# GpSimd announces the end of the projection stage ahead of its rope gathers, and the logits are cleared behind the meeting

## What is computed

```python
z = rmsnorm(x, norm1_g) @ w_in                       # the projection, IN_WIDTH columns
z_q, z_kv, z_kr, z_u, z_v, z_ga, z_gb = jnp.split(z, IN_SPLITS, axis=-1)
q_lat, q_rope, c_kv, k_rope = mla_project(z_q, z_kv, z_kr, pos, ...)
o_lat = attend(q_lat, q_rope, c_kv, k_rope)          # prompt rows: causal; sample rows: over the cache too
...
def step(carry, pages):                              # sample attention, over the pages of the cache
    ck = cache_ckv[pages]
    kr = cache_krope[pages]                          # the rows that the "rope gathers" fetch
    s = mla_scores(q_lat, q_rope, ck, kr)
...
g_logit = (xt @ w_rg) + b_rg                         # router logits: the tile `logits` holds these and e_logit
```

## Time and profile before

| | |
|---|---|
| time, median of 3 runs | 1983.03 us (1980.97 to 1990.81) |
| the profiled execution | 1982.07 us, of which the span is 1980.3 us |
| PE busy | 1816.0 us (92% of the span) |
| DVE, ACT, POOL busy | 750.4, 456.2, 311.3 us |
| PE idle ahead of its first matmul behind the first meeting | 9.10 us |
| POOL's four drains at the meetings | 2.692 to 13.335 us |

### The profile page before, as it was taken

The page is one execution under the profiler, slowest core; times in us unless marked ns, Lnnn a source line. Parts: engine busy times, 40 slices in busy tenths (PEclk is TensorE's granted clock), DMA queues, the critical chain, the costliest instruction groups (busy, mean ns, idle before and its releaser), DMA issues.

```text
span 1980.3 us, 28999 instructions
## 1 busy us (share of the span) xinstructions
PE 1816.0 (92%) x11436; PEld 1238.7 (63%) x11436; DVE 750.4 (38%) x1687; ACT 456.2 (23%) x1002; POOL 311.3 (16%) x430
## 2 busy tenths in 40 slices
PE   7989999999979999999999997999898888898884
PEld 5678888888845656756666664565565555565551
DVE  3343334444423334334555555675322311111116
ACT  3122211111113233223344343212210111111013
POOL 1034311111110000000111103333321211111100
PEclk9999999999989999999999998999798999998997
DMA  7112215565620000026999995544899999999976
GB/s 221 45 66 76 76 60 210 212 214 214 225 87 1 1 1 1 1 65 196 289 304 299 300 303 192 203 143 156 304 408 417 418 415 411 416 405 402 400 326 264
DMA packets 107022, 432.90 MB, mean 219 GB/s; under 512 B 25216, under 2 KB 30752, under 8 KB 77184
## 3 DMA queue, kind: packets, MB, share of 16 engines
q1 hardware_dynamic: 86704, 330.02, 44.6%
q0 software_dynamic: 20160, 101.24, 15.4%
q10 hardware_dynamic: 48, 0.13, 0.0%
HBM read 388.12 MB, written 63.66 MB: 228 GB/s over the span
## 4 chain that ended last, share of the span: by engine, by line
PE 34%; DMA 17%; DVE 2%; ACT 1%; issue 0%; SPq 0%; POOLq 0%; DVEq 0%; ACTq 0%; PEldq 0%
DMA arena<-in_w_up_dram 16%; PE psum L1424 8%; PE psum L1162 6%; PE psum L1292 6%; PE psum L1173 5%; PE psum L1189 3%; PE psum L1443 1%; PE psum L1275 1%; PE psum L1180 1%; PE psum L1317 1%; DMA arena<-in_w_down_dram 1%; DMA arena<-y_rows 0%; DVE arena L2567 0%; PE psum L1282 0%; PE psum L1397 0%
## 5 line engine op out<-in xcount | busy, mean ns | idle before, releaser
L935 PE MATMUL psum<-arena 128*128 128x256 f32 x1792 | 392.6, 379 | 2.5 <-DVE arena L2126 2.1
L935 PEld LDWEIGHTS psum<-arena 128*128 128x128 f32 x1792 | 337.7, 189 | 55.7 <-issue 5.4
L1424 PE MATMUL psum<-arena 128*64 128x256 f32 (+1 forms) x2048 | 280.1, 407 | 65.8 <-DMA arena<-in_w_up_dram 64.0
L1424 PEld LDWEIGHTS psum<-arena 128*64 128x64 f32 (+1 forms) x2048 | 200.3, 153 | 135.5 <-issue 79.5
L1443 PE MATMUL psum<-arena 128*64 128x512 f32 (+1 forms) x512 | 131.3, 595 | 2.5 <-DMA arena<-in_w_down_dram 2.5
L2514 DVE TENSOR_TENSOR arena<-arena,psum 128x256 f32<-128x256 f32 x36 | 15.2, 423 | 310.6 <-ACT arena L1726 310.6
L1162 PEld LDWEIGHTS psum<-arena 128*128 128x128 f32 x1024 | 113.7, 142 | 29.8 <-issue 27.9
L1162 PE MATMUL psum<-arena 128*128 128x128 f32 x1024 | 127.5, 277 | 0.2 <-DVE arena L2204 0.2
L1292 PE MATMUL psum<-arena 128*128 128x512 f32 x256 | 114.3, 599 | 1.3 <-ACT arena L1659 1.3
L1624 ACT COPY arena<-psum 128x512 f32<-128x512 f32 x128 | 72.1, 589 | 171.6 <-PE psum L1162 171.6
L1936 POOL DMA_INDIRECT y_rows<-arena x36 | 40.7, 1131 | 403.5 <-DVE arena L2523 399.7
(11 more groups left out here) (341 smaller groups left out, 2277.0 us busy)
## 6 DMA issues: line engine op xcount, KB each, us to landing
arena<-in_w_gate_dram SPq DMA_DIRECT2D x64, 1024.0 KB, 13.6
arena<-in_w_up_dram SPq DMA_DIRECT2D x64, 1024.0 KB, 20.3
arena<-in_w_down_dram SPq DMA_DIRECT2D x64, 1024.0 KB, 22.3
arena<-in_w_in_dram SPq DMA_DIRECT2D x8, 2048.0 KB, 11.7
z_act<-arena SPq DMA_DIRECT2D x64, 256.0 KB, 2.1
rope_turned<-arena SPq DMA_DIRECT2D x32, 512.0 KB, 4.8
arena<-rope_turned SPq DMA_DIRECT2D x64, 256.0 KB, 11.2
arena<-z_act SPq DMA_DIRECT2D x8, 2048.0 KB, 7.7
```

Source lines behind the costliest of these rows:

```text
L935: last = mm(out[:, 0:256], x[:, k, :], w[:, k, :], start=(k == 0), stop=(k == 3))
L1424: last = mm(bank(2 + u)[rows, DE * x:DE * x + DE], xg_t[u][:, k, rows], w_e[slot][x][:, k, :], start=(k == 0), stop=(k == KD - 1))
```

## The change

POOL's stream: the drain and its increment of `ends` are moved from behind the 32 gathers and the wait for all stores to ahead of the first gather; only the wait `ends >= 4` stays behind. DVE's stream: the clearing of `logits` is moved from ahead of DVE's `stage_end` to behind it.

```diff
             pool.wait_ge(b_mm[0], groups_done(sched, ("G1", NTP))[0])
             pool.wait_ge(b_mm[1], groups_done(sched, ("sR", 0))[1])
+            pool.drain().then_inc(ends, 1)
             for n in range(NCH):
                 if n >= 2:
                     pool.wait_ge(rk_t, n - 1)
                 off = bass.IndirectOffsetOnAxis(ap=page_int[:, n:n + 1].bitcast(U32), axis=0)
                 pool.indirect_dma_start(kr_raw[n % 2].rearrange("p r c -> p (r c)"), None, kr_g, off).then_inc(c_in[n % 2], 16)
             for u in range(2):
                 pool.wait_ge(rk_mv[u], 16 * PRE)
-            stage_end(pool, 1)
+            pool.wait_ge(ends, 4)
```

```diff
                 for p in range(NTP // 2):
                     z_pair(b, p)
+            stage_end(dve, 1)
             step(V.memset(logits, 0.0))
-            stage_end(dve, 1)
```

## The result

The changed kernel takes 1972.12 us (median of 8 runs, 1968.89 to 1978.67) against 1986.85 us (median of 8 runs, 1980.97 to 1991.09) for the kernel before, on the same chips: a ratio of 0.9939, 95% interval 0.9925 to 0.9954. That is 12.1 us faster, between 9.1 and 14.9 us. The ratio is not the quotient of the two medians, which differ by 14.7 us. The forecast was 1973.0 us and 9.8 us.

A forecast was written before the change was run, and what follows sets the result against it. PE's 9.10 us idle at the projection's end, held by POOL alone, was taken as on the path; 7.3 us (meeting) + 2.5 us (clock) = 9.8 us off gave 1973.0 us, range 1968.5 to 1981 us.

The forecast's parts named there:

- Who holds the meeting, and what is late next: End of projection: POOL alone holds PE, DVE is next; PE starts 7.3 us earlier and idles 1.8 us.
- The clock: First K group behind the meeting: clock stays at full, group takes 3.60 instead of 6.11 us, another 2.5 us.
- The rival that it falls anyway: Behind the meeting: the clock still drops, only 7.3 us gained, 1975.7 us or something between; chance 0.16.
- The clearing of the logits: DVE, behind the meeting: its 0.60 us run while PE makes the first two K units, so are covered.
- w_uv: Start of V at 557.0 us: weights land at 555.9 us, margin 1.1 us, costed at nothing.
- The drain ahead of the gathers: POOL, before the first gather: drain of 2.692 to 13.335 us delays it; 22.7 us of cover, costs nothing.
- The gain reaches the end: Everything behind the meeting hangs on counts of engines' work and moves along; second meeting some 9.8 us earlier.
- rival 3: Experts: the 9.8 us are given back at a wait for weights, time 1983.0 us as before; chance 0.07.
- The sum against the median: Whole kernel: 9.8 us off the median of three runs, 1983.03 us, gives 1973.2 us; 1973.0 us predicted.

The follow-up runs named there:

- the early drain: Kernel before, with POOL's drain put between the last gather and the wait for the stores; 0.9979, 4.2 us faster.
- POOL's half: Kernel before, with only POOL's drain and announcement moved ahead of the gathers, logits still cleared ahead of DVE's drain; 0.9969, then 0.9952.
- the kernel that used it up: Changed kernel, with DVE announcing ahead of its last turn and PE waiting at the meeting neither for the others nor for `z_ev`; 0.9940.
- PE kept busy: Kernel before, with 9 idle matmuls on PE between its last product and the meeting, results unused; 0.9999, both times.
- DVE's half: Kernel before, with only the clearing of the logits moved behind the meeting, POOL announcing behind the stores as before; 1.0009.
- DVE late: Changed kernel, with five clearings of the logits ahead of DVE's drain; 0.9978, 4.4 us faster than before.

## Why the prediction was right, and where not

- **Who holds the meeting, and what is late next.** Right: POOL alone before; DVE with the change; the stall 1.78 us (1.8 foreseen), the meeting 7.32 us nearer (7.3). The split of POOL's lateness into stores and drain is shown by the early drain: 2.8 us for the drain. DVE's drain lasted 1.551 us where the prediction took 0.017 to 0.322 us, at no cost, since it ran beside the transposes and ended 0.06 us behind them.
- **The clock.** Right in the stage for this stall: 2.40 us (2.5 foreseen), in all three traces. The rival that it falls anyway did not happen at 1.78 us, but did once of two at 2.47 us, so its chance was not misplaced. The prediction rested on one row, the stall of 2.12 us at 585.44 us in which the clock stayed at full. At or behind that same stall it fell in four of the 14 traces, so the row was one outcome of two, and proved less than I took from it. The Trainium skill, "TensorE: Matmul & The Clock Gate", section "What's actually happening", says that the window runs free of the kernel; the two executions of POOL's half, equal in the stall and different in the clock, agree with this. What I drew from it, that even a stall of 1.8 us can be followed by a group at half rate, no trace shows: it did not happen in three executions with 1.78 us. That the 2.4 us reach the end isn't shown: the kernel with the clock alone kept measured 0.2 us, twice, and lost 1.7 us of the 2.4 again some 28 us later in both traces.
- **The clearing of the logits.** Right: hidden behind the meeting, 0.69 us of stall ahead of it when POOL is early, nothing when POOL is late. The measured times leave room for more than 0.69 us (some 4 us between POOL's half and the whole change), which the traces of the stage don't account for.
- **w_uv.** Right: no wait in the changed kernel, and a margin of about 1 us, shown by the kernel that used it up.
- **The drain ahead of the gathers.** Right that it costs nothing; its size was missed. I reckoned with 2.7 to 13.3 us and a first gather 3 us later. It lasted 0.055 us, and the gather started at 260.65 us, 0.15 us later than before once the 2.0 us are taken off by which this trace is late as a whole. The drains that I took for it, 2.692 and 13.335 us, stand behind indirect DMAs, and this one has none before it.
- **The gain reaches the end.** Right in sign and roughly in size: 12.1, 12.3 and 11.9 us for a sum of 9.7 us. It wasn't given back, so rival 3 is out. The 0.6% measured lie beyond 0.5%, where the prediction had put 0.38, and not within it, where it had put 0.59. The term that the sum did not have is in the rest of the kernel, where I took all stretches as moved without change. The changed kernel's attention was at its shortest in all three traces, 3.4 us under the one of before. But kernels with a late meeting had 342.4 and 342.5 us too, and some with an early one had 345.8 us, so the cause isn't the early meeting as such. Its length follows the shares of the clock that are missing in it (5.1 us against 8.5 us). Why they were fewest in all three traces of the changed kernel stays open. Whether the moment of the start of this stage fixes the clock's fall in it, or chance did, would need many traces of each kernel, and one program (PE kept busy) gave both 342.5 and 347.4 us.
- **The sum against the median.** The median of before was higher with 8 runs (1986.85 us) than with the 3 shown (1983.03 us), so the forecast of the time (1973.0 us) was closer than that of the gain.

No version beats the changed kernel by more than can be measured; going on at this meeting means an earlier `w_uv` first.

## What to carry to other kernels

An engine should announce at a meeting when its last work that others must wait for is done, and wait there for itself later: a background job that stands between the two, here a DRAM store that lands 6 us behind the last product, holds every engine for nothing. When the holder is freed, look who is next (here DVE, then ACT, then a weight load) and reckon the gain to that one only. A stall that drops TensorE's clock costs more than its length in its stage, but whether that part arrives at the end has to be measured, since the clock's falls elsewhere vary by several us from one execution to the next. And one trace in which the clock outlasts a stall does not show that it always will.

## What the runs showed of the hardware that was not expected

- POOL's drain lasted 0.055 us with no indirect DMA before it in the stream, 5.813 us directly behind an indirect DMA (at 533.2 us), and 2.692 us some 20 us behind one. At the second meeting of the kernel before it lasted 13.335 us, directly behind an indirect DMA that took 13.1 us to land. I have no cause for the 2.692 us.
- With a stall of 2.47 us the granted clock fell in one execution and stayed at full in another of the same program; where it fell, PE had been at work again for 1.3 us. With stalls of 5.7 to 9.1 us it fell 3.5 to 4.3 us behind the last product, in four traces (before, DVE's half, drain early, DVE late); with 1.78 us and less it stayed at full in six traces.
- At or behind one stall of 2.12 or 2.13 us, the same in all 14 traces (PE waits for ACT at L1057), the clock fell in four traces and stayed at full in ten. Each time the shares missing to full came to 1.7 us.
- The length of the prompt's attention, 342.3 to 347.4 us for the same code, follows the clock's missing shares over it, 5.1 to 10.2 us.
